# Last projection and routing in one block, and the combination with the last norm in rows of tokens

## The reference, cut to what matters

```python
mix = (gate_a * (o_a @ w_a) + gate_b * (o_b @ w_b)) @ w_o
x = x + mix
h = rms_norm(x, norm_ffn_g)
g_logits = h @ w_group + b_group          # 4 groups
e_logits = h @ w_expert + b_expert        # 32 experts, 8 in a group
# best group, its best two experts, weight = p_group * softmax(top two)
y = (silu(h @ w_gate_e) * (h @ w_up_e)) @ w_down_e   # for each chosen expert
x = x + weight[0] * y[0] + weight[1] * y[1]
return rms_norm(x, norm_final_g)
```

## Time and profile before

| | us |
|---|---|
| median of 3 runs | 3281.94 |
| lowest and highest | 3273.8, 3284.9 |
| the profiled execution, as timed | 3287.82 |
| its span, first to last instruction | 3285.7 |
| TensorE busy | 3059.9 |
| VectorE busy | 1399.6 |
| ScalarE busy | 865.1 |
| GpSimd busy | 259.2 |

### The profile page before, as it was taken

The page is one execution under the profiler, slowest core; times in us unless marked ns, Lnnn a source line. Parts: engine busy times, 40 slices in busy tenths (PEclk is TensorE's granted clock), DMA queues, the critical chain, the costliest instruction groups (busy, mean ns, idle before and its releaser), DMA issues. The chain is left out here.

```text
span 3285.7 us, 37758 instructions
## 1 busy us (share of the span) xinstructions
PE 3059.9 (93%) x14882; PEld 2313.0 (70%) x14882; DVE 1399.6 (43%) x2162; ACT 865.1 (26%) x1355; POOL 259.2 (8%) x278
## 2 busy tenths in 40 slices
PE   6999999899888999999999999999999898879996
PEld 4888888777643788888888887888788664443334
DVE  3646454545566464654333524333422473221112
ACT  3112111332254322223222313212323450011111
POOL 1000000001000100001000101000100441012220
PEclk8999999999898999999999999999999989879997
DMA  6323323211000355542232212232322101438883
GB/s 237 115 101 117 121 99 132 79 54 63 14 1 13 127 226 181 222 158 98 90 102 88 91 52 74 83 112 81 105 99 97 63 1 48 179 136 346 347 343 117
DMA packets 78490, 395.22 MB, mean 120 GB/s; under 512 B 17568, under 2 KB 20000, under 8 KB 51744
## 3 DMA queue, kind: packets, MB, share of 16 engines
q1 hardware_dynamic: 66848, 385.12, 31.9%
q0 software_dynamic: 11520, 8.43, 0.8%
HBM read 443.82 MB, written 16.78 MB: 140 GB/s over the span
## 5 line engine op out<-in xcount | busy, mean ns | idle before, releaser
L717 PE MATMUL ps<-h_high_ffn,weights_high_ffn 128*128 128x512 f32 (+1 forms) x1696 | 624.7, 368 | 8.3 <-issue 3.8
L718 PE MATMUL ps<-h_low_ffn,weights_high_ffn 128*128 128x512 f32 (+1 forms) x1696 | 623.5, 368 | 0.0
L719 PE MATMUL ps<-h_high_ffn,weights_low_ffn 128*128 128x512 f32 (+1 forms) x1696 | 623.1, 367 | 0.0
L717 PEld LDWEIGHTS ps<-h_high_ffn,weights_high_ffn 128*128 128x128 f32 x1696 | 320.1, 189 | 64.3 <-issue 8.9
L718 PEld LDWEIGHTS ps<-h_low_ffn,weights_high_ffn 128*128 128x128 f32 x1696 | 320.3, 189 | 52.7
L719 PEld LDWEIGHTS ps<-h_high_ffn,weights_low_ffn 128*128 128x128 f32 x1696 | 320.0, 189 | 52.6
L717 PE MATMUL ps<-hidden_high_ffn,weights_high_ffn 128*128 128x512 f32 (+1 forms) x880 | 327.5, 372 | 20.3 <-DVE weights_low_ffn L852 13.0
L801 ACT ACTIVATE weights_high_ffn<-weights 128x2048 fp32r<-128x2048 f32 (+4 forms) x160 | 243.8, 1524 | 343.3 <-PE ps L719 275.6
L718 PE MATMUL ps<-hidden_low_ffn,weights_high_ffn 128*128 128x512 f32 (+1 forms) x880 | 326.2, 371 | 0.0
L719 PE MATMUL ps<-hidden_high_ffn,weights_low_ffn 128*128 128x512 f32 (+1 forms) x880 | 325.9, 370 | 0.0
L852 DVE TENSOR_TENSOR weights_low_ffn<-weights,weights_high_ffn 128x2048 fp32r<-128x2048 f32 (+4 forms) x160 | 289.5, 1809 | 83.1 <-ACT weights_high_ffn L801 81.8
(11 more groups left out here) (420 smaller groups left out, 4485.7 us busy)
## 6 DMA issues: line engine op xcount, KB each, us to landing
weights<-in_ffn_gu SPq DMA_DIRECT2D x88, 1024.0 KB, 5.0
big<-in_w_exp_gu SPq DMA_DIRECT2D x32, 2048.0 KB, 13.6
scratch_ffn<-in_w_mod SPq DMA_DIRECT2D x35, 1536.0 KB, 6.4
weights<-in_ffn_d SPq DMA_DIRECT2D x24, 768.0 KB, 4.2
weights<-in_w_in SPq DMA_DIRECT2D x16, 1024.0 KB, 4.8
weights<-in_ffn_d SPq DMA_DIRECT2D x24, 640.0 KB, 3.9
weights<-in_w_exp_dn SPq DMA_DIRECT2D x15, 1024.0 KB, 14.0
hbuf<-in_w_exp_dn SPq DMA_DIRECT2D x12, 1024.0 KB, 16.6
```

Of the source, the lines that this page charges most:

```text
L717: pe.matmul(out, wh, xh, start=(k == 0), stop=False)
L718: pe.matmul(out, wh, xl, start=False, stop=False)
L719: mm = pe.matmul(out, wl, xh, start=False, stop=(k == n - 1))
```

## The change

`project_residual`, `norm` and `route` become one function, `project_and_route`, in the block of `merge`. The projection is written out without a loop, and VectorE adds each tile when its own product is done. ScalarE multiplies each tile of x by the gain into `gained`, with no root. TensorE makes the logits of `gained`, one tile behind the additions, adding up over tiles in PSUM. The roots are applied to the logits (VectorE) and to the turned rows of tokens as they are copied out (ScalarE, scale). They aren't spread over partitions any more. `xy` itself is turned into rows of tokens and copied back in place, between the counting products and the offsets. The slab, table and expert loads are issued from this function.

`combine` works in rows of tokens: ScalarE weighs the first result of blocks 0 to 2, GpSimd adds it to x, VectorE adds the weighed second result; VectorE does both for block 3. ScalarE squares with a running sum along the row (`accum_out`) and takes the root, VectorE inverts it and multiplies by root and gain, and each block of 128 tokens is stored as it is. The gain comes as a new 128x1024 table, loaded at the start of the block. The last `norm` and `store_output` are gone, and `out` has tokens as rows.

```diff
+                for n in range(2, 4):
+                    sync.wait_ge(fm["wo_product"].sem, o0 + 2 * n - 2)
+                    sync.dma_start(ring.buf[:, n % 2, :], io["w_o2"][n]).then_inc(ring.landed[n % 2], 16)
+                    if n == 2:
+                        for c in ready:
+                            sync.wait_ge(c.sem, c.at)
+                        for dst, name, landed in router_tables():
+                            sync.dma_start(dst, name).then_inc(landed.sem, 16)
+                load_expert(sync, 0)
+                load_expert(sync, 1, down=False)
+                load_expert(sync, 2, down=False)
+                sync.wait_ge(fm["wo_product"].sem, o0 + KD)
+                load_expert(sync, 3)
+                load_expert(sync, 1, gate_up=False)
+                load_expert(sync, 2, gate_up=False)
                 for i in range(TT):
                     sync.wait_ge(turn_ev[0].sem, v0 + i + 1)
                     sync.dma_start(io["token_rows"][i * P:(i + 1) * P, :], hT[:, i, :]).then_inc(rows_stored.sem, 16)
...
+                clear_squares(vector, NX)
+                for m in range(KD):
+                    vector.wait_ge(fm["wo_product"].sem, o0 + m + 1)
+                    vector.tensor_tensor(xy[:, m, 0:NX], ps[:, m % 4, :], xy[:, m, 0:NX], ALU.add).then_inc(fm["wo_added"].sem, 1)
+                    if m < KD - 1:
+                        add_square(vector, m, NX)
                 vector.wait_ge(tables.sem, t0 + 16 * len(ROUTER))
+                invert_roots(vector, NX)
+                vector.wait_ge(nm["rooted"].sem, nm["rooted"].at + 2)
...
+                vector.wait_ge(proj_done[0].sem, p0 + 1)
+                one(vector.tensor_tensor(L, logits, over(inverse[:, 1, 0:TT], NG + NE), ALU.mult))
+                one(vector.tensor_tensor(L, L, rows(rb, NG + NE), ALU.add))
...
+                for m in range(KD):
+                    if m == KD - 1:
+                        scalar.activation(warm[:, 0:1], eps[:], ACT.Sqrt)
+                    scalar.wait_ge(fm["wo_added"].sem, r0 + m + 1)
+                    square_tile(scalar, m, xy[:, m, 0:NX], NX)
+                    scalar.activation(gained[:, m, :], xy[:, m, 0:NX], ACT.Copy, scale=gain[:, m, 0:1]).then_inc(scaled.sem, 1)
+                token_roots(scalar, NX)
+                scalar.wait_ge(nm["rooted"].sem, nm["rooted"].at + 2)
                 for i in range(TT):
                     scalar.wait_ge(turn_done[0].sem, u0 + i + 1)
-                    scalar.activation(hT[:, i, :], turned(i), ACT.Copy).then_inc(turn_ev[0].sem, 1)
+                    scalar.activation(hT[:, i, :], turned(i), ACT.Copy, scale=inverse[:, 1, i:i + 1]).then_inc(turn_ev[0].sem, 1)
                 scalar.wait_ge(dve_chain.sem, mark[0])
                 scalar.activation(gs[:, :, 8:8 + NG], gs[:, :, 8:8 + NG], ACT.Exp).then_inc(exp_done[0].sem, 1)
+                for i in range(TT, 2 * TT):
+                    scalar.wait_ge(turn_done[0].sem, u0 + i + 1)
+                    scalar.activation(rows_of(i - TT), turned(i).rearrange("p (k n) -> p k n", k=KD), ACT.Copy).then_inc(turn_ev[0].sem, 1)
                 scalar.wait_ge(dve_chain.sem, mark[2])
...
+                def choose(k):
+                    pe.wait_ge(scaled.sem, z0 + k + 1)
+                    for i in range(TT):
+                        mm = pe.matmul(logits[:, i, :], gained[:, k, i * P:(i + 1) * P], wr[:, k, :],
+                                       start=(k == 0 and i == 0), stop=(k == KD - 1 and i == TT - 1))
+                    if k == KD - 1:
+                        mm.then_inc(proj_done[0].sem, 1)
+
+                def turn(i, src):
+                    if i >= 2:
+                        pe.wait_ge(turn_ev[0].sem, v0 + i - 1)
+                    for k in range(KD):
+                        mm = pe.transpose(turned(i)[:, k * P:(k + 1) * P], src[:, k, i % TT * P:(i % TT + 1) * P], ident[:])
+                    mm.then_inc(turn_done[0].sem, 1)
+
...
+                for m in range(KD):
+                    n = m // 2
+                    wv = ring.view(n % 2, 2, KD, P)
+                    if m % 2 == 0:
+                        pe.wait_ge(ring.landed[n % 2], 16 * (n0[n % 2] + n // 2 + 1))
+                    if m >= 4:
+                        pe.wait_ge(fm["wo_added"].sem, r0 + m - 3)
+                    for k in range(KD):
+                        mm = pe.matmul(ps[:, m % 4, :], wv[:, m % 2, k, :], U[:, k, 0:NX], start=(k == 0), stop=(k == KD - 1))
+                    mm.then_inc(fm["wo_product"].sem, 1)
+                    if m == 2:
+                        pe.wait_ge(tables.sem, t0 + 16 * len(ROUTER))
+                    if m >= 2:
+                        choose(m - 2)
+                choose(KD - 2)
+                sum_squares(pe, NX, KD)
+                choose(KD - 1)
                 for i in range(TT):
+                    turn(i, gained)
...
                 mm.then_inc(counted.sem, 1)
+                for i in range(TT, 2 * TT):
+                    turn(i, xy)
 
                 pe.wait_ge(dve_chain.sem, mark[3])
-                pe.matmul(ps[0:NE, 1, 2 * P:3 * P], before[0:NE, 0:NE], extra[0:NE], start=True, stop=False)
...
+                for c in ready:
+                    gpsimd.wait_ge(c.sem, c.at)
+                gpsimd.wait_ge(nm["sums"].sem, nm["sums"].at + 1)
                 for b in range(2):
                     gpsimd.memset(xin(b), 0.0).then_inc(rows_cleared.sem, 1)
                 gpsimd.wait_ge(rows_cleared.sem, 2)
...
+        square = [big[:, (2 * TT + b) * D:(2 * TT + b + 1) * D] for b in range(2)]
+        gain = work[:, 0:D]
+        sums = inverse[:, 0, 0:TT]
...
+                sync.dma_start(gain, io["final_gain"]).then_inc(tables.sem, 16)
...
+                    sync.wait_ge(scaled.sem, s0 + i + 1)
+                    sync.dma_start(io["out"][i * P:(i + 1) * P, :], Y[:, 0, i, :]).then_inc(out_done.sem, 16)
+                sync.wait_ge(out_done.sem, 16 * TT)
...
+                def first_share(i):
+                    scalar.wait_ge(y_read[i].sem, 32)
+                    scalar.activation(Y[:, 0, i, :], Y[:, 0, i, :], ACT.Copy, scale=share[:, 0, i:i + 1]).then_inc(weighed.sem, 1)
+                first_share(0)
+                first_share(1)
                 for i in range(TT):
+                    if i == 0:
+                        first_share(2)
                     scalar.wait_ge(added[0].sem, a0 + i + 1)
                     if i >= 2:
-                        scalar.wait_ge(nm["sums"].sem, nm["sums"].at + i - 1)
-                    scalar.activation(squares[i % 2].rearrange("p (k n) -> p k n", k=KD), xy[:, :, i * P:(i + 1) * P], ACT.Square)\
+                        scalar.wait_ge(nm["squared"].sem, q0 + i - 1)
+                    scalar.activation(square[i % 2], Y[:, 0, i, :], ACT.Square, accum_out=sums[:, i:i + 1]).then_inc(nm["squared"].sem, 1)
+                    scalar.wait_ge(nm["squared"].sem, q0 + i + 1)
+                    scalar.activation(sums[:, i:i + 1], sums[:, i:i + 1], ACT.Sqrt, bias=eps[:, 0:1], scale=1.0 / D)\
+                        .then_inc(nm["rooted"].sem, 1)
+
+            @block.gpsimd
+            def _(gpsimd):
+                for i in range(TT - 1):
+                    gpsimd.wait_ge(weighed.sem, w0 + i + 1)
+                    gpsimd.tensor_tensor(rows_of(i), rows_of(i), Y[:, 0, i, :].rearrange("p (k n) -> p k n", k=KD), ALU.add)\
+                        .then_inc(added[1].sem, 1)
 
             @block.vector
             def _(vector):
                 def weigh(i):
-                    vector.wait_ge(y_read[i].sem, 32)
-                    step(vector.tensor_scalar(Y[:, 0, i, :], Y[:, 0, i, :], share[:, 0, i:i + 1], None, ALU.mult))
+                    if i == TT - 1:
+                        vector.wait_ge(y_read[i].sem, 32)
+                        step(vector.scalar_tensor_tensor(rows_of(i), Y[:, 0, i, :].rearrange("p (k n) -> p k n", k=KD),
+                                                         share[:, 0, i:i + 1], rows_of(i), ALU.mult, ALU.add))
+                        steps_done(vector)
+                    else:
+                        vector.wait_ge(added[1].sem, b0 + i + 1)
+                    vector.scalar_tensor_tensor(Y[:, 0, i, :].rearrange("p (k n) -> p k n", k=KD),
+                                                Y[:, 1, i, :].rearrange("p (k n) -> p k n", k=KD), share[:, 1, i:i + 1],
+                                                rows_of(i), ALU.mult, ALU.add).then_inc(added[0].sem, 1)
+
+                def finish(i):
+                    vector.wait_ge(nm["rooted"].sem, r0 + i + 1)
+                    step(vector.reciprocal(inverse[:, 1, i:i + 1], sums[:, i:i + 1]))
                     steps_done(vector)
...
+                    vector.scalar_tensor_tensor(Y[:, 0, i, :], Y[:, 0, i, :], inverse[:, 1, i:i + 1], gain, ALU.mult, ALU.mult)\
+                        .then_inc(scaled.sem, 1)
+
+                vector.wait_ge(tables.sem, t0 + 16)
```

(13 more changed lines are left out.)

215 lines of the change are left out of this document (38 added, 177 removed).

## The result

The changed kernel takes 3249.26 us (median of 4 runs, 3244.93 to 3255.52) against 3283.42 us for the kernel before beside it (4 runs, 3273.8 to 3289.13): a ratio of 0.9909, 95% interval 0.9886 to 0.9932. That is 34.2 us less; the interval alone reaches from 22 to 37. The forecast was 3252.3 us and 29.6 us less.

What follows compares the result with a forecast made beforehand. TensorE was busy for 3059.9 of 3285.7 us, but the edit was priced along the chains before and behind the experts. Front 21.9 - 0.3 - 2.1 = 19.5, plus tail 10.1, is 29.6 off 3281.94: 3252.3 us, range 3243 to 3264.

Steps and rivals of the forecast that it cites:

- Last product's end: Projection on TensorE: 1.4 us of gaps lost, five logit groups add 4.9 us, so the last product ends at 2858.2.
- the gaps: Between the projection's four loop halves on TensorE: straight code would lose all 1.4 us of them.
- Last product to logits: Remaining groups and sums on TensorE: VectorE starts on the logits at 2863.1 instead of 2885.01, 21.9 us gained.
- Turned tokens: Routing: four groups of xy transposes behind the counts delay the chain by 2.1 us at TensorE's full clock.
- My rival: Routing on TensorE: the clock falls before the counts, 4.2 us less gained, 3256.5 us; chance 0.2.
- Loads: Table loads hide under product 3 (1 to 2 us if uncovered); token row stores hide by some 13 us.
- Experts: Expert stage: shifts as a whole, so a microsecond won before it is one at the end.
- the rival in which the gain is given back: Late tables or row stores, or other buffers at the first experts: a 10 us stall gives 3262; chance 0.1.
- Tail: Behind the experts: VectorE and GpSimd times added up, end at 3275.6 instead of 3285.7, 10.1 us gained.
- Overlap of the two engines: Tail rival: GpSimd and VectorE overlap, so the tail gains 13.0 us and the kernel takes 3249.4; chance 0.12.
- Slower: Projection rival: small products between large ones drop TensorE's clock to 1.2 GHz, giving 3301 us; chance 0.03.
- Whole time: Whole kernel: 29.6 us less than the median before, 3252.3 us; chance 0.55.

Runs made afterwards that it cites:

- after, again: The changed kernel with no edit, run and profiled a second time: 3248.24 us, ratio 0.9905 to the kernel before.
- logits_behind: Changed kernel with the sums and all eight logit groups issued behind the last product, in the same block: 3261.2 us (one run).
- barrier_behind: Changed kernel with sums and all logits behind the last product and an all-engine barrier between product and sums: 3247.38 us (one run).
- front_only: Changed kernel with combination, last norm and output layout of the kernel before, and no xy transposes: 3257.58 us, ratio 0.993.
- three_buffers: Changed kernel with three PSUM buffers instead of two for the transposed blocks, order of work unchanged: 3237.92 us (one run).
- turn_late: Changed kernel with the xy transposes moved ahead of the routing's last product, into a TensorE wait: 3241.08 us, ratio 0.9877.
- gain_behind: Changed kernel with the final norm's gain table loaded behind the first block's result rows instead of ahead of all: 3248.45 us (one run).

## Why the prediction was right, point by point

- **Last product's end.** Forecast 63.6 us after the first product, measured 61.5, and 62.7 in after, again, whose first product started as slowly as that of before (0.62 and 0.61). So 1.1 of the difference is that clock, and 0.9 is mine. The groups cost what I said: between profiles that start alike, the last product ends 4.8 us (62.7 - 57.8, logits_behind) and 4.7 us (61.5 - 56.9, barrier_behind) later with five groups than without, forecast 4.9, or 0.9 to 1.0 each. The term that was too small is the gaps: the straight code alone, without groups, brings the end from 60.1 to 57.8 and from 58.9 to 56.9, 2.0 to 2.2 us and not 1.4.
- **Last product to logits.** Forecast 4.9, measured 4.8 (4.6 in after, again). The gain at the logits, forecast 21.9, is 22.9 and 23.2 between profiles whose first product started alike; most of the excess is the gaps.
- **Turned tokens.** Forecast -2.1 and -0.3 for the extra operation. Measured -2.9 for both between the two first profiles, and -3.3 for the transposes alone against front_only, which has the extra operation too. Here a step failed in the profile of the result: the clock. I held it at 1.00 through to the transposes because TensorE had hardly idled. The counts did run at 1.00, but the transposes began at 0.60, and the rows for the gather were turned at 0.67 (the windows above). My rival put the fall ahead of the counts; it fell ahead of and behind them. In after, again the clock is 1.00 there, and the term comes out as worked: 4.22 us for the transposes, forecast 4.4, and 1.8 us against front_only, forecast 2.1. So its working was sound at the clock that it assumed, and the fall, which I held unlikely, came in three of four profiles. three_buffers shows that buffers are a smaller part, turn_late that the transposes need not be there. What decides whether the clock is up at this place stays open.
- **Loads.** Hidden, as forecast, but with nothing to spare at the tables. The first weight load of the first logit group stands 0.74 us behind the load ahead of it, released by the last table (0.91 in after, again), where 0.24 is usual. TensorE's products lose little by it: that group takes 0.91 us to the next product instead of 0.81. The seven issues took from 2802.02 to 2805.42, half of the third product's time. The row stores land late, queued behind the weights, and the gather does not wait for them. The changed kernel's issues of these stores (count, KB, median us from issue to landing; 4.2 us before), and TensorE's largest class of waits in the experts, as in the earlier trace rows:

```profile
token_rows<-work SPq DMA_DIRECT2D x4, 512.0 KB, 10.2
```

```profile
PE ps L2803 <- issue: 21.1, 23, 1.0
```

- **Experts.** Forecast to shift as a whole: 319.4 and 319.1 us. Over all 14 profiles it is 316.9 to 320.8 with no pattern by front, so the rival in which the gain is given back (a stall of 10 us) is out, and a change of a microsecond or two could not be seen.
- **Tail.** Forecast 10.1 from the sum of both engines' times, measured 11.0. The first ScalarE weighing starts 15.65 us after the last copy, where VectorE's stood at 14.20 before and ScalarE's at 14.30 in gain_behind, so the gains' table costs 1.35 to 1.45, forecast 1.2. GpSimd's addition is 2.33, not 2.41. Hand-overs and reciprocals, forecast 1.2, come to 0.3. The store from the last step's end takes 3.06, forecast 3.2.
- **Overlap of the two engines.** This rival would have given 3249.4 us, and the median is 3249.26, yet it is refuted: steps of 3.34 us beside an addition, and a tail that is 3.8 us shorter when GpSimd adds nothing, where by overlap I expected it 1 to 3 us longer. A total that agrees with a rival says nothing for it. The trace agrees with the Trainium skill, "SBUF — State Buffer", section "SBUF: two separate sides", on a shared port held by one engine at a time; the case in the earlier trace rows that bore it out was tiny, and it carried over to 128x1024.
- **Slower.** Refuted by the granted clock of 1.00 over 2817 to 2840. But the argument that I gave against it was wrong. I said that the old logits ran at half clock because their stretch began after a pause; logits_behind has a pause of only 0.66 us and runs them at half clock too. The clock held because the groups stood between products: their place is all that logits_behind changes, and in after, too, the one group that stands behind the sums takes 1.34 us instead of 0.98.
- **Whole time.** The forecast of 29.6 us less met 34.2 by medians and 33.0 in the stretches. The stretches exceed it by 3.4 us: 2.2 in the front (21.7 for 19.5, of which 1.2 is the clock of the first product), 0.9 in the tail, 0.3 in the experts. Some of the agreement is luck: in the front the gaps gave more than forecast and the turned tokens cost more, and the median of a few runs could lie several us off, since the start of the projection alone scatters by 17.

## What to carry to other kernels

Where a reduction over rows (here the root of a norm) only scales a product's result, take the product of the raw rows and scale its small result: the pass, the spreading and both barriers leave the path, 13.8 us here (30.3 to 16.5). Put small f32 products one group at a time between large ones instead of in a row behind them, another 7 to 8 us here, with the 4.7 us of added work beside the products already paid. And put work that nobody needs yet into an engine's wait rather than ahead of the next link of a chain. Before giving VectorE's additions to GpSimd, look for VectorE steps that lengthen while GpSimd runs: here VectorE alone was 3.8 us faster.
